# Strassen-like block sums of weights, formed in DRAM by accumulating DMAs

## The reference

```
x = x + rmsnorm(merged @ w_mix_out, g_mix_post)          # 2048 x 2048
kv = mem_n @ w_mem_kv                                    # 2048 x 4096, the right half are the values
x = x + rmsnorm(memory_xattn(...), g_mem_post)
a = h @ w_ffn_in                                         # 2048 x 11264
x = x + rmsnorm((gelu(gate) * up) @ w_ffn_out, g_ffn_post)   # 5632 x 2048
```

## Time and profile before

| | |
|---|---|
| median of 3 runs | 1768.47 us (1768.03 to 1768.61) |
| span of the profiled execution | 1766.9 us (no separate time is given for it; the median is 1.6 us above the span) |
| PE busy | 1755.8 us, 99% |
| DVE busy | 1224.9 us, 69% |
| ACT busy | 940.6 us, 53% |
| POOL busy | 63.1 us, 4% |
| DMA | 330.90 MB, mean 187 GB/s |

### The profile page before, as it was taken

How to read it: one execution, slowest core, us unless ns; L and a number is a source line. 1 busy time by engine, 2 the same in 40 slices (tenths; PEclk the granted TensorE clock), 3 DMA queues, 4 the chain that set the end, 5 groups by cost and what they waited for, 6 DMA issues and landing times.

```text
span 1766.9 us, 25116 instructions
## 1 busy us (share of the span) xinstructions
PE 1755.8 (99%) x8930; PEld 1480.5 (84%) x8930; DVE 1224.9 (69%) x1727; ACT 940.6 (53%) x1287; POOL 63.1 (4%) x128
## 2 busy tenths in 40 slices
PE   9999999999999999999999999999999999999998
PEld 7888888888888888888888888888888888888886
DVE  6555565655456876576665477777777778898887
ACT  7555555665446655444555574444444444455554
POOL 4000000000000110000000100000000000000002
PEclk9999999999999999999999999999999999999999
DMA  8456554555556565556444555555555555646555
GB/s 296 149 192 192 150 181 142 178 170 160 206 194 233 171 223 178 167 191 214 166 145 167 190 206 199 184 183 184 187 189 190 190 183 184 198 168 213 183 202 191
DMA packets 192872, 330.90 MB, mean 187 GB/s; under 512 B 17655, under 2 KB 44199, under 8 KB 191399
## 3 DMA queue, kind: packets, MB, share of 16 engines
q1 hardware_dynamic: 191254, 318.48, 54.7%
q10 hardware_dynamic: 1552, 11.54, 1.7%
HBM read 325.81 MB, written 4.19 MB: 187 GB/s over the span
## 4 chain that ended last, share of the span: by engine, by line
PE 98%; DVE 1%; DMA 1%; ACT 0%; SPq 0%; issue 0%; DVEq 0%; ACTq 0%
PE bank L1313 18%; PE bank L714 11%; PE bank L716 11%; PE bank L715 11%; PE bank L1315 9%; PE bank L1046 7%; PE bank L1048 7%; PE bank L1047 7%; PE bank L1142 3%; PE bank L1239 3%; PE bank L1240 2%; PE bank L1143 2%; PE bank L928 2%; PE bank L739 1%; PE bank L929 1%; PE bank L951 1%
## 5 line engine op out<-in xcount | busy, mean ns | idle before, releaser
L2060 DVE TENSOR_TENSOR wlo<-raw,whi 128x1024 fp32r<-128x1024 f32 (+1 forms) x480 | 587.1, 1226 | 418.0 <-ACT whi L1466 282.3
L1466 ACT ACTIVATE whi<-raw 128x1024 fp32r<-128x1024 f32 x312 | 330.1, 1059 | 370.2 <-PE bank L1315 209.6
L1313 PE MATMUL bank<-actA,whi 128*128 128x512 f32 x1344 | 472.0, 394 | 0.0
L1315 PE MATMUL bank<-actA,wlo 128*128 128x256 f32 x1344 | 380.1, 283 | 0.0
L1313 PEld LDWEIGHTS bank<-actA,whi 128*128 128x128 f32 x1344 | 252.4, 188 | 58.3
L1452 ACT ACTIVATE whi<-raw 128x1024 fp32r<-128x1024 f32 (+1 forms) x167 | 174.8, 1050 | 150.6 <-PE bank L716 61.1
L1315 PEld LDWEIGHTS bank<-actA,wlo 128*128 128x128 f32 x1344 | 252.7, 188 | 0.0
L714 PE MATMUL bank<-whi,actA 128*128 128x512 f32 x460 | 187.4, 407 | 0.0
L716 PE MATMUL bank<-whi,actA 128*128 128x512 f32 x460 | 181.5, 395 | 0.0
L715 PE MATMUL bank<-wlo,actA 128*128 128x512 f32 x460 | 181.5, 394 | 0.0
L1998 ACT ACTIVATE whi<-raw 128x1024 fp32r<-128x1024 f32 x105 | 111.2, 1061 | 101.2 <-PE bank L1048 83.4
(11 more groups left out here) (380 smaller groups left out, 2737.9 us busy)
## 6 DMA issues: line engine op xcount, KB each, us to landing
raw<-in_w_ffn_in SPq DMA_DIRECT2D x88, 1024.0 KB
raw<-in_w_in SPq DMA_DIRECT2D x46, 1024.0 KB
raw<-in_w_ffn_out SPq DMA_DIRECT2D x84, 512.0 KB, 4.8
raw<-in_w_mem_kv SPq DMA_DIRECT2D x18, 1024.0 KB
raw<-in_w_attn_br SPq DMA_DIRECT2D x16, 1024.0 KB
raw<-in_w_mem_q SPq DMA_DIRECT2D x16, 1024.0 KB
raw<-in_w_mem_o SPq DMA_DIRECT2D x16, 1024.0 KB
raw<-in_w_mem_kv SPq DMA_DIRECT2D x28, 512.0 KB, 4.4
```

The source lines that it names most:

```text
L1313: pe.matmul(dst[:, :], whi[:, s, o:o + P], actA[:, :, kt, :], start=(kt == 0), stop=False)
L1315: mm = pe.matmul(dst[:, 0:S], wlo[:, s, o:o + P], actA[:, 0, kt, :], start=False, stop=(kt == KD - 1))
L1466: act.activation(whi[:, ks % AHEAD, 0:w], raw[:, c, ks % 2, 0:w], ACT.Copy).then_inc(hi_done, 1)
L2060: dve.tensor_tensor(wlo[:, vs % AHEAD, 0:w], raw[:, c, vs % 2, 0:w], f32(whi[:, vs % AHEAD, 0:w]), ALU.subtract).then_inc(lo_done, 1)
```

## The change

The sums of weight blocks are no longer made in SBUF. A DRAM tensor `weight_sums` holds f4, f5, f7, f6 for each of 14 groups. POOL's queue copies w11 and w12 into the places of f4 and f5, w21 and w22 into those of f7 and f6 (two copies of 1 MB), and adds to them with accumulating DMAs of 0.5 MB each: w12 to f4, w22 to f5, then f4 to f6, then f6 to f7. Steps are tied to `lo_done`, 8 units apart: 14 steps in the pool projection and attention stages for MIXED and VALUES, 18 steps in the FFN for FOUT. In each step POOL first waits for the DMAs of the step before. SP loads sums like any other block, after `w_summed`; the planner goes, each unit has its own half slot in turn.

Groups become 2 in MIXED, 2 in each half of VALUES, 4 in each half of FOUT. Orders change, and the order of forms in a group too. In FOUT the token sums of all 4 groups are made once. PE waits for the four token sums one by one. In MIXED the roles of the banks are permuted (`M_AT`).

```diff
-    G0, G1 = 3, 4
-    FORMS = ("w11", "w22", "f4", "w21", "f5", "f6", "f7")
+    GF = 4
+    FORMS = ("w11", "w21", "f7", "f4", "f6", "w22", "f5")
+    LEAD = 4
-    PAIR0 = pair_units(0, G0, "s" * 17 + EACH * G0 + "s" * 3)
-    PAIR1 = pair_units(1, G1, "F" + "s" * 4 + EACH[1:] + EACH * (G1 - 1) + "s" * 8)
-    VALUES = (pair_units(0, 1, "s" * 4 + EACH + "s" * 4, KD // 2)
-              + pair_units(1, 1, "F" + "s" * 4 + EACH[1:] + "s" * 4, KD // 2))
+    PAIR0 = pair_units(0, GF, "s" * 9 + EACH * GF + "s" * 3)
+    PAIR1 = pair_units(1, GF, "F" + "s" * 4 + EACH[1:] + EACH * (GF - 1) + "s" * 8)
+    VALUES = sum((pair_units(p, GV, "F" + "sFF" * 4 + "sFFF" + "sFF" + "ss", KD // 2) for p in range(2)), [])
-    MIXED = pair_units(1, GM, "ssss" + EACH + "ssss", KD // 2)
+    MIXED = pair_units(1, GM, "ss" + "FFFs" * 4 + "FF" + "ss", KD // 2)
...
+    SUM_FORMS, TOKEN_SUMS = ("f4", "f6", "w22", "f5"), (0, 1, 3, 2)
+    M_AT = (4, 5, 2, 3, 0, 1, 6, 7)
...
+        def block_load(base, n, u, w, col, sums, landing):
+            p, g, f = u
+            sp.wait_ge(lo_done, base + n - 2 * RAW_SLOTS + 1)
+            if f in SUMS:
+                sp.wait_ge(w_summed, sums_ready(sums + g))
+                src = weight_sums[sums + g, :, :, SUM_AT[f], :]
+            else:
+                k, c = block_at(u)
+                src = w[:, k:k + 2, col + c * NC:col + (c + 1) * NC]
+            h = half_of(base, n)
+            sp.dma_start(raw_half(h).rearrange("p (k n) -> p k n", n=NC), src).then_inc(landing[h], 16)
...
+        def weight_sum_step(i, first, groups, unit):
+            pool.wait_ge(lo_done, unit)
+            if issued[0] > 0:
+                pool.wait_ge(w_summed, 16 * issued[0])
+            g = first + i // 2
+            if i // 2 < groups:
+                w, c, k = summed_group(g)
+                if i % 2 == 0:
+                    copy(weight_sums[g, :, :, 0:2, :]..., w[:, k:k + 2, c:c + 2 * NC])
+                    copy(weight_sums[g, :, :, 2:4, :]..., w[:, k + 2:k + 4, c:c + 2 * NC])
+                else:
+                    add(weight_sums[g, :, :, SUM_AT["f4"], :], w[:, k:k + 2, c + NC:c + 2 * NC])
+                    add(weight_sums[g, :, :, SUM_AT["f5"], :], w[:, k + 2:k + 4, c + NC:c + 2 * NC])
+            if i >= 2:
+                if i % 2 == 0:
+                    add(weight_sums[g - 1, :, :, SUM_AT["f6"], :], weight_sums[g - 1, :, :, SUM_AT["f4"], :])
+                else:
+                    add(weight_sums[g - 1, :, :, SUM_AT["f7"], :], weight_sums[g - 1, :, :, SUM_AT["f6"], :])
...
+        weight_sum_steps(V_YP, 0, 2, 0, EARLY_SUMS, 8)
+            weight_sum_steps(V_ATT + 24 * i + 18, 2 + 3 * i, 5 + 3 * i, 0, EARLY_SUMS, 8)
+        weight_sum_steps(V_FIN + 8, 0, 2 * LATE_SUMS + 2, F_SUMS, LATE_SUMS, 8)
...
-                if FOUT[n] == (0, 0, "w22"):
-                    pe.wait_ge(xs_lo, 4)
-                if FOUT[n] == (1, G0, "w22"):
-                    pe.wait_ge(xs_lo, 8)
+                if FOUT[n][:2] == (0, 0) and FOUT[n][2] in SUM_FORMS:
+                    pe.wait_ge(xs_lo, SUM_FORMS.index(FOUT[n][2]) + 1)
...
             if n + AHEAD < NU:
-                f_hi_of(n + AHEAD)
+                block_hi(V_FOUT, n + AHEAD, b_loaded, LEAD)
+            if n in (7, 10, 12, 14):
+                xs_split((7, 10, 12, 14).index(n))
...
             if n + AHEAD < NU:
-                f_lo_of(n + AHEAD)
-            if n + SUM_LEAD < NU and FOUT[n + SUM_LEAD][2] in SUMS:
-                f_add(n + SUM_LEAD)
+                lo(V_FOUT + n + AHEAD, V_FOUT + n + AHEAD)
             if n < 8:
                 up_job(NF - 1, n)
-            elif n < 15:
-                xs_make(0, G0, n - 8, 0)
+            if n == 2:
+                dve.wait_ge(w_used, V_FOUT)
+            if n in (2, 6, 8, 9, 10, 11, 12, 13):
+                token_sums(gT, XF, GF, (2, 6, 8, 9, 10, 11, 12, 13).index(n), xs_step, xs_full)
+            if n in (9, 11, 13, 15):
+                i = (9, 11, 13, 15).index(n)
+                sum_low(XS[TOKEN_SUMS[i]], XF[TOKEN_SUMS[i]], i, xs_hi, xs_lo)
```

More of the change, by code:

```diff
@@ L409, in raw_half @@
         return raw[:, h // 2, h % 2, :]
[L411 to L447, removed]
@@ L449, in hybrid_layer, with half_of, landed @@
-    HOME, LANDED, FREE, BLOCKS, SUM_OF, _ = plan(FOUT, V_FOUT, 4)
-    V_HOME, V_LANDED, V_FREE, V_BLOCKS, V_SUM_OF, V_LEAVES = plan(VALUES, V_VAL, 4)
-    M_HOME, M_LANDED, M_FREE, M_BLOCKS, M_SUM_OF, M_LEAVES = plan(MIXED, V_MIXP, 4)
+    def half_of(base, n):
+        return (base + n) % (2 * RAW_SLOTS)
+    def landed(n, lead=0):
+        return 16 * ((n - lead) // (2 * RAW_SLOTS) + 1)
     def visits(v):
         skipped = sum(1 for base, after in ((V_MIXP, V_MKV), (V_VAL, V_MQ)) if v >= after
-                      for q in range(base // 2 + 2, after // 2) if q % RAW_SLOTS == v // 2 % RAW_SLOTS)
+                      for q in range(base // 2, after // 2) if q % RAW_SLOTS == v // 2 % RAW_SLOTS)
@@ L568, in _ @@
         w_kv, w_mix = rows("w_mem_kv"), rows("w_mix_out")
[L569 to L583, removed]
@@ L587, in _ @@
+        for n, u in enumerate(MIXED):
+            block_load(V_MIXP, n, u, w_mix, 0, M_SUMS, mb_loaded)
         for j in range(KD // 4):
[L588 to L591, removed]
+            load(V_MKV // 2 + j, (V_MKV // 2 + j) % RAW_SLOTS, w_kv[:, 4 * j:4 * j + 4, 0:NC], NC)
         with sp.Fori(1, ND) as i:
             column(V_MKV // 2 + 4 * i, w_kv, i * NC, s=V_MKV // 2 % RAW_SLOTS)
-        for j in range(2):
-            k = 2 * VALUES[2 * j][1]
-            load(V_VAL // 2 + j, V_VAL // 2 + j, w_kv[:, k:k + 4, ND * NC:(ND + 1) * NC], NC)
@@ L680, in _, with summed_group, copy @@
             last.then_inc(consts_ok, 1)
-        with pool.Fori(0, ND) as i:
+        def summed_group(i):
+            if i < V_SUMS:
+                return rows("w_mix_out"), 2 * NC, 4 * i
+            if i < F_SUMS:
+                p, g = (i - V_SUMS) // GV, (i - V_SUMS) % GV
+                return rows("w_mem_kv"), (ND + 2 * p) * NC, 4 * g
+            p, g = (i - F_SUMS) // GF, (i - F_SUMS) % GF
+            return rows("w_ffn_out"), 2 * p * NC, 4 * g
+        issued = [0]
+        def copy(dst, src):
+            pool.dma_start(dst, src).then_inc(w_summed, 16)
+            issued[0] += 1
@@ L683, in _, with weight_sum_steps @@
+        def weight_sum_steps(base, i0, i1, first, groups, per):
+            for i in range(i0, min(i1, 2 * groups + 2)):
+                weight_sum_step(i, first, groups, base + per * (i - i0))
+        weight_sum_steps(V_YP, 0, 2, 0, EARLY_SUMS, 8)
+        for i in range(ND):
             for t in range(TT):
                 pool.wait_ge(acc_out[t], U_ATT + 4 * i + 3)
-                ya = bufY[:, t, bass.ds(i * NC, NC)]
+                ya = bufY[:, t, i * NC:(i + 1) * NC]
                 pool.tensor_tensor(ya, ya, gp_sb[:, t, :], ALU.mult).then_inc(mp_ok, 1)
+            weight_sum_steps(V_ATT + 24 * i + 18, 2 + 3 * i, 5 + 3 * i, 0, EARLY_SUMS, 8)
@@ L1048, in split3, with plain @@
             return pe.matmul(dst, lo, wh, start=False, stop=last)
-        def plain(u, v, x, t, opens, closes):
+        def plain(u, v, x, t, opens, closes, at_=range(8)):
             p, kp, c = u
-            dst = bank[((B11, B12), (B21, B22))[t][c]]
+            dst = bank[at_[((B11, B12), (B21, B22))[t][c]]]
             for kk in range(2):
@@ L1057, in plain, with formed @@
             return mm
-        def formed(u, v, x, xs, opens, closes):
+        def formed(u, v, x, xs, opens, closes, at_=range(8)):
             p, g, f = u
-            dst = bank[{"w11": Q1, "w21": B11, "w22": B12, "f7": B21, "f4": Q5, "f6": Q6, "f5": Q7}[f]]
+            dst = bank[at_[{"w11": Q1, "w21": B11, "w22": B12, "f7": B21, "f4": Q5, "f6": Q6, "f5": Q7}[f]]]
             for kk in range(2):
@@ L1438, in hi @@
                 return
+            if isinstance(v, int):
+                for base, units, landing in ((V_MIXP, MIXED, mb_loaded), (V_VAL, VALUES, vb_loaded)):
+                    if base <= v < base + len(units):
+                        block_hi(base, v - base, landing)
+                        return
             c = (vs // 2) % RAW_SLOTS
@@ L1683, in prewarm, with column @@
             act.activation(warm[:, :], var[:, n, :], ACT.Sqrt)
-        def column(base, u, n, dst, norm, job, y=None, ahead=()):
+        def column(base, u, n, dst, norm, job, y=None, ahead=(), squares=sc[0][:, :]):
             for k in range(8):
@@ L2550, in _ @@
                 value_combine(0, 8)
[L2551 to L2553 removed]
+            lo(V_VAL + n + AHEAD, V_VAL + n + AHEAD)
         value_combine(1, 7)
@@ L2863, in combine @@
             op.then_inc(y_step, 1)
-        for n in range(4, SUM_LEAD):
-            if FOUT[n][2] in SUMS:
-                f_add(n)
         for n in range(NU):
```

350 lines of the change are left out of this document (99 added, 251 removed).

## The result

The changed kernel takes 1772.09 us (median of 12 runs, 1770.73 to 1773.86) where the one before takes 1768.31 us (12 runs, 1767.82 to 1768.8). The ratio is 1.0022, with a 95% interval of 1.0014 to 1.0029: it is slower by 3.8 us. The profiled execution's span grows from 1766.9 to 1770.1 us, so the trace holds 3.2 us of it.

A forecast was written before the change was run, and what follows sets the result against it. TensorE's matmuls were taken to bound the kernel: -5.6 - 0.36 + 0.5 + 4.9 = -0.6 us, giving a span of 1766.3 us and a median of 1767.9 us, range 1762.5 to 1778.

The forecast's parts named there:

- The matmuls: TensorE, all stages with formed groups: groups go from 10 to 14, so 24 matmuls at 0.2323 us go, -5.6 us.
- The first unit of MIXED: Start of MIXED: its first unit writes banks 4 and 5, already free, so PE's 0.36 us wait goes.
- Sums of tokens for MIXED at twice the length: DVE, before MIXED: token sums made a column earlier at twice the length fit in DVE's gaps, no cost.
- MIXED, no cost: Start of MIXED: w11, now unit 2, gets its bank back from the last memory split with 0.8 us margin.
- Change of halves in VALUES: Between the halves of VALUES: a plain unit waits for banks freed by DVE's combinations, one stall of 0.5 us.
- The output stage: First half of FOUT: PE waits for DVE's weight splits and third token sum at w22, +4.9 us (4.0 to 6.3).
- The sums in DRAM: GpSimd's copies and accumulating adds: finished a stage early and hidden in free DMA engine time, priced at nothing.
- the lower end: DMA engines: copies and adds cost only their reading at 396 GB/s, 16 us per group, which fits.
- the upper: DMA engines: copies and adds priced from store and load landing times, 50 us per group, which does not fit.
- the 19 us: FFN: DMA engine time left free by the loads per group of two steps (45 us).
- the 12 us of slack: Weight loads: time a load can be late, being issued when the unit seven before is split, some 12 us.
- rival (A): Sums' transfers push weight loads back; a microsecond of PE waiting in a third of 32 steps, 1779 us, chance 0.22.

The follow-up runs named there:

- the last kernel: Changed kernel with later summed units in FOUT, sums' steps moved, reordered VectorE turns and MIXED units, VALUES halves closing with three plain units: 1762.49 us (0.9969).

## Why the prediction was wrong

It forecast 1767.9 us and no measurable change; the kernel is slower by 0.22%. By its own steps:

**The matmuls, -5.6 us.** Right: 24 fewer by the page, and the last kernel gets 5.7 us.

**The first unit of MIXED, -0.36 us.** Its wait is gone and 0.5 us with it (from the first of the eight small matmuls ahead of it to its own first one, 1.16 us became 0.63).

**Sums of tokens for MIXED at twice the length, "nothing".** Wrong by 0.4 us. Attention without transfers is only 0.14 us shorter than before, not 0.5. In the last column of attention's output VectorE's scaling of memv comes later behind the longer token operations, and PE's four small matmuls that read it start late: at 581.03, 0.46 us after the matmul before them where it was 0.23, and they take 0.38 us where it was 0.29. That is 0.3 of the 0.4 us, read from the trace; no run has it alone.

**MIXED, no cost.** There was one: a low split is 0.24 us late behind three formed units, which costs 0.5 us by the starts (0.64 us between starts for 0.23, and 0.33 for the next). Moving one unit took it away.

**Change of halves in VALUES, +0.5 us.** Right in place, cause and time to 0.2: the two gaps at the wait lose 0.69 us by starts, and removing it brought 0.66. The whole stretch lost only 0.27 us against its matmuls; what it gained elsewhere I did not trace.

**The output stage, +4.9 us.** The wait itself was as worked out: at w22, on the low part of the third token sum, behind a small one at unit 16. VectorE's order was that of the text, and

```profile
1565.19 1.21 DVE L2309 TENSOR_TENSOR xs<-xf,xs 128x1024 fp32r<-128x1024 f32 x1
```

ends at 1566.4. The forecast had 1568.4 in a stage that begins at 1523.14; it began at 1521.00, so the chain of sixteen operations came out within 0.2 us. By starts, PE loses 4.28 us at w22 and 0.84 around it to waits, 5.1 in all. **This is the step that failed, though not in its wait**: the term took a late operand as costing its lateness only. After 4.1 us without a matmul the granted clock fell to 0.50 for some 3 us, 1.64 us more. The run with later units removes both, the run with the wait cut up removes the clock's part alone, and the wait put elsewhere brings it back. The Trainium skill, TensorE: Matmul & The Clock Gate, "Part 1: The HAM clock gate (the "warmup" mystery)", says that the clock is set by how busy the engine has been recently; the traces agree (0.50 after 4.1 and 6.9 us without a matmul, 1.00 throughout with four waits of at most 1.7).

**The sums in DRAM, "nothing".** The second step that failed, by 1.7 us in the changed kernel. Price and size: GpSimd's queue took 17.0% of 16 engines' span, 301 us for 14 groups or 21.5 us a group. That is near the lower end (16 us) and far from the upper (50), but above the 19 us that I had called free. In the FFN, where I made that sum, it cost nothing all the same: the stretch takes 703.53 us with them and 703.5 without, though the share of the engines went from 0.57 to 0.99 there and not towards 0.70. What failed is the step from the free time per group and the 12 us of slack, worked out for half-slot loads, to all loads. In attention the loads are of 1 MB and come in bursts; the kernel before shows around the first place

```profile
245.00:250.00 5.00, 5.00 (x30) 4.35 (x29) 4.68 (x19) 2.38 (x4) 0.00 (x0) 1.00 0.95 312
```

There one step's additions push a load of w_in back, ACT's split waits for it up to 3.3 us, ACT's copies of v_sb stand behind that split in its queue, and PE waits for those. Only some 2.0 us of ACT's wait were free. The loss was 1.26 us at the first place and 0.44 at the second. This is rival (A) in kind, but at two of the 32 steps, not a third. The rule that I set against the change (the Trainium skill, DMA: Bandwidth & Descriptors, "Issuing engines are not separate DMA queues"), that GpSimd's DMAs run on the same 16 engines, the traces bear out: with 97.4% of the engines' time on GpSimd's queue the loads had 0.9%.

**The sum.** -5.6 - 0.5 + 0.4 + 1.7 + 0.6 (MIXED) + 0.3 (VALUES) - 0.3 (keys) + 5.1 + 1.6 = +3.3 us, against 3.2 in the two profiled executions. The 0.3 us that the keys gained I did not trace. The forecast missed by 3.8 us of span (and 0.4 us more in the median, which stands 2.0 us above the span here and not 1.6): the clock 1.6, the late loads 1.7, MIXED 0.6 and the token sums 0.4, less 0.5 of small gains. Each was small beside the wait that I had worked out; the prediction had put them at nothing or not looked for them.

## What to carry to other kernels

Price a wait of the engine that sets the time by what happens after it as well: a wait listed with 4.1 us cost 5.9, while the same work behind shorter waits (4.5 us in all by starts) kept the clock; if operands must be late, let them be late in pieces. Also price it by the distance of starts, not by the listed idle time: waits listed with 0.24 to 0.44 us cost 0.5 to 0.7. The listed idle time starts only when the matmul before, listed with 0.39 us, has ended, 0.16 us after the next one was due, and the gap behind the wait is longer too. Where a background transfer is added, the free time per period says little; look for the load with the least slack, what stands behind its consumer in that engine's queue, and keep the transfers off it.

## What the runs showed of the hardware

- An accumulating DRAM-to-DRAM transfer of 512 KB lands in 10.1 us where a plain one of the same size takes 8.7, and with both sides in the sums' buffer 17.4 against 12.0. It costs all 16 engines 1.3 us more. From 240 to 245 us additions had 97.4% of the engines' time and the loads beside them 0.9%, and 92 GB/s moved in all; with plain transfers in their place the loads had 20.4%, and 210 GB/s moved.
- After 4.1 us without a matmul the granted clock was still 1.00 for the first four matmuls and fell during the fifth; after 6.9 us it had fallen during the wait, and the matmuls were slow from the first one on (0.60 us to the second start, 0.43 from there). The losses were nearly alike, 1.64 and 1.88 us.
- The first matmul after a wait is followed by the next one 0.31 to 0.34 us later instead of 0.23, at a granted clock of 1.00.
